# A four-layer hybrid transformer in fp32 on one core: the passage between sublayers in two halves of the tokens, with the last panel scaled in PSUM

## The chip, the cores and the metric

The kernel runs on one core of one Trainium2 chip. The metric is the device time of one execution in microseconds (us), median of the runs. The engines are TensorE (PE in the rows, PEld its weight loads), VectorE (DVE), ScalarE (ACT), GpSimd (POOL) and SyncE (SP), which here only starts DMAs.

## The reference

`h` is 512 tokens of 1024 features. Four layers each have a mixer (two kinds of attention with sparse or windowed keys, one stick-breaking attention) and a feed-forward part with a short convolution. Each of the eight sublayers is wrapped alike, and the change touches only the wrapping:

```python
def rms_norm(x, g):
    x32 = x.astype(jnp.float32)
    y = x32 * lax.rsqrt(jnp.mean(x32 * x32, axis=-1, keepdims=True) + RMS_EPS)
    return (y * g.astype(jnp.float32)).astype(x.dtype)
...
for layer in range(DEPTH):
    u = rms_norm(h, norm_g[layer, 0])
    u = mixer(u)                                # nsa, stick-breaking, swa, nsa; ends in "@ w_out"
    h = h + rms_norm(u, norm_g[layer, 1])
    u = conv_ffn(rms_norm(h, norm_g[layer, 2]), ...)  # ends in "@ w_down"
    h = h + rms_norm(u, norm_g[layer, 3])
```

## The kernel before

Features lie on the 128 partitions and tokens along the free dimension, so `h` is 8 chunks (`c`) of 128 x 512. Every fp32 product is made from three: weights and inputs are split into a rounded high part and a low part (`w_hi`, `w_lo`, `xh`, `xl`), and TensorE adds hi x hi, lo x hi and hi x lo. Weights come in units of 128 x 1024 through a ring of four buffers: SP loads `w_raw`, ScalarE rounds it (`split_hi`), VectorE subtracts (`split_lo`), TensorE uses it. A unit of an input projection covers two chunks and four banks of PSUM. A panel is four banks (512 output features) and takes four units; panels alternate between the two halves of PSUM, and `panel_free` waits until the panel two back was taken out (`evac_v`, `evac_s`).

The work around the change is the passage from the end of one sublayer (its output projection, two panels) to the first panel of the next. Each engine runs a list written out by hand, tied by semaphores. In order:

- `act_squares` squares each bank of the projection, `dve_take_u` copies each bank into `u` (`mix_u` or `ffn_u`), `pool_sum_squares` adds the first panel's squares, and `pe_post` sums over the partitions by products with `ones`, the last one after the projection's last bank.
- `act_rn` makes `rn` = (mean + eps)^-0.5 by Ln and Exp.
- `dve_update` goes through the eight chunks: scale `u` by the weight of the norm and by `rn` (line 454, into `dh`), add to `h` (line 460), and, one chunk behind, the low part `xl` = h * g - `xh` (line 440, `low`). Between them lies ScalarE's work of `act_update`: `xh`, the rounded h * g (line 472), and the square of `h` (line 477), which `pool_h_squares` adds up on GpSimd (lines 484 and 488).
- `first_panel` begins the next sublayer with what is there: it takes chunk by chunk, eight products with `xh` as soon as the chunk's `xh` is there (lines 319, 320), then four with `xl` (line 323). The division by the norm of `h` is left until after the products (`rb`), so `pe_rsum`, the sum over the squares, comes only after the first panel.
- The weights' units go on meanwhile: the fourth unit of the first panel is split on ScalarE behind the last square and on VectorE behind the last copy, ahead of the update.

There are eight such updates. Seven lead into another sublayer; the eighth has no `g_pre`, ends the kernel, and each chunk of `h` is written out by a DMA.

## Time and profile before

| | us |
|---|---|
| median of 3 runs | 2765.12 (2763.9 to 2768.2) |
| profiled execution, its own time | 2761.04 |
| its span, first to last instruction | 2759.3 |
| TensorE busy in it | 2629.6 |
| VectorE busy | 1721.9 |
| ScalarE busy | 1194.5 |
| GpSimd busy | 351.1 |

The times of single instructions come from the profiled execution. Starts in the rows are us from the span's start. A busy time counts an instruction from its start to its end, and TensorE's instructions overlap, so the distance from one start to the next tells more than a duration.

### The profile page before, as it was taken

The page shows a single profiled execution, that of the slowest core. Times are in us where ns is not written, and L with a number is a line of the kernel's source. Part 1 is how long each engine was busy: PE and PEld are TensorE (multiplying, and loading weights), DVE is VectorE, ACT ScalarE, POOL GpSimd, SP SyncE. Part 2 cuts the span into 40 slices and gives each one's busy share as a digit, 9 for nine tenths or more (in the row PEclk, how much of TensorE's full clock was granted, in tenths as well). Part 3 has the DMA queues.
Part 4 walks back from the last instruction along what each step waited for, and adds up shares of the span by engine and source line. Part 5 has one row for each costly group of instructions (what it writes and reads, how often), then busy time and mean ns, then how long its engine had stood idle before and what let it go on. Part 6 is the DMA issues. An engine that isn't in the chain of part 4 may idle for free.

```text
span 2759.3 us, 38755 instructions
## 1 busy us (share of the span) xinstructions
PE 2629.6 (95%) x13424; PEld 2201.1 (80%) x13424; DVE 1721.9 (62%) x2888; ACT 1194.5 (43%) x2117; POOL 351.1 (13%) x298
## 2 busy tenths in 40 slices
PE   8989999999999999999998999999999899999997
PEld 6878878888878787888877878888778788788886
DVE  7468857765262857767345767763476686676643
ACT  4356634443232744444235644443233665444431
POOL 1012211110010002111010021110011121211100
PEclk9989999999999999999999999999999999999999
DMA  4300023333223012332322023333333000233331
GB/s 159 122 31 2 2 69 99 99 92 98 85 96 100 16 39 77 100 99 84 107 74 69 14 87 100 99 92 99 96 100 100 9 2 24 77 103 96 99 96 49
DMA packets 62054, 210.93 MB, mean 76 GB/s; under 512 B 8672, under 2 KB 10464, under 8 KB 61920
## 3 DMA queue, kind: packets, MB, share of 16 engines
q1 hardware_dynamic: 61920, 209.14, 24.3%
q8 instruction: 84, 1.38, 0.2%
q14 instruction: 50, 0.41, 0.0%
HBM read 207.02 MB, written 2.10 MB: 76 GB/s over the span
## 4 chain that ended last, share of the span: by engine, by line
PE 83%; DVE 11%; ACT 3%; issue 2%; DMA 0%; DVEq 0%; POOL 0%; SPq 0%; ACTq 0%; POOLq 0%
PE psum L298 20%; PE psum L300 20%; PE psum L299 20%; PE psum L960 5%; PE psum L950 2%; DVE h L460 2%; PE psum L815 2%; PE psum L817 2%; PE psum L816 2%; PE psum L940 1%; DVE xl L440 1%; PE psum L319 1%; DVE qs L991 1%; PE psum L939 1%; PE psum L1701 1%
## 5 line engine op out<-in xcount | busy, mean ns | idle before, releaser
L298 PE MATMUL psum<-xh,w_hi 128*128 128x512 f32 x1736 | 682.2, 393 | 3.0 <-DVE xl L1204 3.0
L300 PE MATMUL psum<-xl,w_hi 128*128 128x512 f32 x1736 | 677.6, 390 | 0.0
L299 PE MATMUL psum<-xh,w_lo 128*128 128x512 f32 x1736 | 677.6, 390 | 0.0
L258 DVE TENSOR_TENSOR w_lo<-w_raw,w_hi 128x1024 fp32r<-128x1024 f32 x226 | 280.2, 1252 | 515.8 <-ACT w_hi L252 514.2
L252 ACT ACTIVATE w_hi<-w_raw 128x1024 fp32r<-128x1024 f32 x226 | 235.5, 1057 | 578.4 <-PE psum L300 456.0
L298 PEld LDWEIGHTS psum<-xh,w_hi 128*128 128x128 f32 x1736 | 327.3, 189 | 72.9 <-issue 5.8
L299 PEld LDWEIGHTS psum<-xh,w_lo 128*128 128x128 f32 x1736 | 327.3, 189 | 69.3 <-issue 1.9
L300 PEld LDWEIGHTS psum<-xl,w_hi 128*128 128x128 f32 x1736 | 327.0, 188 | 68.6
L615 DVE TENSOR_TENSOR w_lo<-w_raw,w_hi 128x1024 fp32r<-128x1024 f32 x160 | 209.2, 1308 | 253.8 <-ACT w_hi L611 253.8
L298 PE MATMUL psum<-ah,w_hi 128*128 (+1 forms) x704 | 277.1, 394 | 0.0
L300 PE MATMUL psum<-al,w_hi 128*128 (+1 forms) x704 | 274.0, 389 | 0.0
L299 PE MATMUL psum<-ah,w_lo 128*128 (+1 forms) x704 | 273.9, 389 | 0.0
L611 ACT ACTIVATE w_hi<-w_raw 128x1024 fp32r<-128x1024 f32 x160 | 168.5, 1053 | 234.9 <-PE psum L300 234.9
L960 PE MATMUL psum<-v,pt 128*128 128x64 f32 x1504 | 213.3, 272 | 25.4 <-DVE pt L1063 25.3
L960 PEld LDWEIGHTS psum<-v,pt 128*128 128x128 f32 x1504 | 203.3, 194 | 42.1 <-DVE pt L1063 37.1
L585 POOL TENSOR_TENSOR cv<-cv 128x512 f32<-128x512 f32 x88 | 133.7, 1519 | 787.0 <-ACT cv L539 784.3
L1114 ACT ACTIVATE scores<-scores,mins 128x256 f32<-128x256 f32 (+1 forms) x320 | 171.4, 538 | 29.6 <-DVE mins L1008 22.5
L534 ACT ACTIVATE cv<-xo,conv_b,conv_w 128x512 f32<-128x512 f32 x176 | 129.2, 805 | 95.5 <-DVE xo L558 95.5
L567 DVE SCALAR_TENSOR_TENSOR cv<-xo,conv_w,cv 128x512 f32<-128x512 f32 x176 | 169.5, 1003 | 0.6 <-DVE xo L558 0.6
L1008 DVE CUSTOM_DVE_ANT_0 scores<-psum,tb 128x256 f32<-128x256 f32 (+1 forms) x320 | 148.8, 468 | 25.0 <-PE psum L940 22.8
L299 PEld LDWEIGHTS psum<-ah,w_lo 128*128 128x128 f32 x704 | 132.2, 188 | 29.3 <-issue 1.9
L298 PEld LDWEIGHTS psum<-ah,w_hi 128*128 128x128 f32 x704 | 132.2, 188 | 29.2 <-issue 1.9
(180 smaller groups left out, 4011.1 us busy)
## 6 DMA issues: line engine op xcount, KB each, us to landing
w_raw<-w_up SPq DMA_DIRECT2D x176, 512.0 KB, 3.6
w_raw<-w_down SPq DMA_DIRECT2D x88, 512.0 KB, 3.6
w_raw<-nsa_in SPq DMA_DIRECT2D x56, 512.0 KB, 4.1
w_raw<-sb_in SPq DMA_DIRECT2D x24, 512.0 KB, 3.7
w_raw<-nsa_out SPq DMA_DIRECT2D x16, 512.0 KB, 3.6
w_raw<-swa_in SPq DMA_DIRECT2D x10, 512.0 KB, 4.4
w_raw<-sb_out SPq DMA_DIRECT2D x8, 512.0 KB, 3.6
w_raw<-swa_out SPq DMA_DIRECT2D x8, 512.0 KB, 3.8
```

The source lines that it names most:

```text
L252: nc.scalar.activation(w_hi[:, u % RING, :], w_raw[:, u % RING, :], ACT.Copy).then_inc(hi_done, 1)
L258: nc.vector.tensor_tensor(w_lo[:, u % RING, :], w_raw[:, u % RING, :], w_hi[:, u % RING, :].bitcast(F32), ALU.subtract).then_inc(split_don ...
L298: nc.tensor.matmul(bank(p, o), wh[:, k, o, :], xhi(k), start=(first and k == 0), stop=False)
L299: nc.tensor.matmul(bank(p, o), wl[:, k, o, :], xhi(k), start=False, stop=False)
L300: mm = nc.tensor.matmul(bank(p, o), wh[:, k, o, :], xlo(k), start=False, stop=(last and k == 1))
L567: marks.append(ch.then(nc.vector.scalar_tensor_tensor(cv[:, o, :], xo[:, o, 1:T + 1], conv_w[:, 1, bass.ds(cc, 1)], cv[:, o, :], ALU.mult, ...
L585: nc.gpsimd.tensor_tensor(cv[:, 2 + a, :], cv[:, a, :], cv[:, 2 + a, :], ALU.mult).then_inc(prod_done, 1)
L611: nc.scalar.activation(w_hi[:, u % RING, :], w_raw[:, u % RING, :], ACT.Copy).then_inc(hi_done, 1)
L615: nc.vector.tensor_tensor(w_lo[:, u % RING, :], w_raw[:, u % RING, :], w_hi[:, u % RING, :].bitcast(F32), ALU.subtract).then_inc(split_don ...
L960: mm = nc.tensor.matmul(psum[:, 6 + job % 2, i * DH:(i + 1) * DH], pt[:, s % 2, j * P:(j + 1) * P], vt[b][:, k0 + j, bass.ds(it * DH, DH)] ...
L1008: x = nc.vector.tensor_tensor_reduce(out=sp_[:, s % 4, 0:nk * P], in0=psum[:, s % 4, 0:nk * P], in1=bias, scale=1.0, scalar=3e38, op0=ALU. ...
L1114: nc.scalar.activation(sp_[:, s % 4, 0:nk * P], sp_[:, s % 4, 0:nk * P], ACT.Exp, scale=-1.0, bias=mins[:, c:c + 1], accum_out=rsums[:, c: ...
```

## The change

The passage is arranged anew:

- The last bank's square, the sum over the partitions, Ln and Exp are made in two halves of 256 tokens. The mean of the squares comes from `ones` that hold 1/D, so Ln needs no scale. The halves lie in two banks (`mean_half`).
- Chunk 0's `xh` no longer comes from ScalarE. ScalarE prepares h * g_pre of the old `h` ahead of the second panel's squares (`hg_done`); VectorE scales `u` by `gg` (the product of both norms' weights, made once at the start) and by `rn` and adds the prepared part, rounding as it writes `xh`, half by half. `first_panel` takes chunk 0's products with `xh` in halves.
- VectorE's order in `dve_update` is new: `xh` of chunk 0 in halves, update of chunk 1, update of chunk 0, both low parts, then for each chunk from 2 on the update and its low part. An update is line 454's scaling and line 460's add, the second waiting for the first.
- The second panel is not copied out: chunks 4 to 7 are scaled in place in PSUM, and the panel counts as taken out (`evac_v`) at the end of the update.
- VectorE's split of the first panel's fourth unit moves from ahead of the update to behind the update of chunk 4. ScalarE's stays.

```diff
+TH = T // 2
...
+        gg = small("gg", [P, 2 * DEPTH - 1], F32)
...
-        mix_u = Space(A_, T_)("mix_u", [P, DC, T], F32)
-        ffn_u = Space(16 * K, 32 * K)("ffn_u", [P, DC, T], F32)
+        mix_u = Space(A_, T_)("mix_u", [P, 4, T], F32)
+        ffn_u = Space(24 * K, 32 * K)("ffn_u", [P, 4, T], F32)
...
+        sqa_done = sem("sqa_done")
+        hg_done = sem("hg_done")
+        xa_done = sem("xa_done")
+        gg_done = sem("gg_done")
-        dh_done = sem("dh_done")
...
                 for k in range(2):
                     c = 2 * j + k
-                    pe.wait_ge(xh_done, 8 * n + c + 1)
-                    pe.wait_ge(split_done, u + 1)
-                    for o in range(4):
-                        nc.tensor.matmul(bank(p, o), wh[:, k, o, :], xh[:, c, :], start=(c == 0), stop=False)
-                        nc.tensor.matmul(bank(p, o), wl[:, k, o, :], xh[:, c, :], start=False, stop=False)
+                    parts = [(0, T)] if c or n == 0 else [(0, TH), (TH, T)]
+                    for lo, hi in parts:
+                        if hi < T:
+                            pe.wait_ge(xa_done, n)
+                        else:
+                            pe.wait_ge(xh_done, 8 * n + c + 1)
+                        pe.wait_ge(split_done, u + 1)
+                        for o in range(4):
+                            if o == 3 and hi < T:
+                                pe.wait_ge(r_done, 2 * n)
+                            nc.tensor.matmul(bank(p, o)[:, lo:hi], wh[:, k, o, :], xh[:, c, lo:hi], start=(c == 0 and lo == 0), stop=False,
+                                             skip_group_check=True)
+                            nc.tensor.matmul(bank(p, o)[:, lo:hi], wl[:, k, o, :], xh[:, c, lo:hi], start=False, stop=False,
+                                             skip_group_check=True)
                     pe.wait_ge(x_ready, 8 * n + c + 1)
                     for o in range(4):
-                        mm = nc.tensor.matmul(bank(p, o), wh[:, k, o, :], xl[:, c, :], start=False, stop=(c == DC - 1))
+                        mm = nc.tensor.matmul(bank(p, o), wh[:, k, o, :], xl[:, c, :], start=False, stop=(c == DC - 1),
+                                              skip_group_check=True)
                 mm.then_inc(units_done, 1)
 
         def after_rsum(pe, p, u0, n, by_token):
...
-                act.wait_ge(s_chain, ch.then(nc.scalar.activation(rt[:], bank(p, 2)[:, 0:TC], ACT.Ln, bias=eps[:], scale=1.0 / D)))
+                act.wait_ge(s_chain, ch.then(nc.scalar.activation(rt[:], bank(p, 2)[:, 0:TC], ACT.Ln, bias=eps[:])))
...
-            a = nc.scalar.activation(rb[:], bank(p, 3), ACT.Ln, bias=eps[:], scale=1.0 / D)
+            a = nc.scalar.activation(rb[:], bank(p, 3), ACT.Ln, bias=eps[:])
...
             if o == 2:
                 panel_free(pe, p + 1)
                 pe.wait_ge(ss_done, s + 1)
-                nc.tensor.matmul(bank(p + 1, 3), ones[:], ss[:], start=True, stop=False)
+                for a in range(2):
+                    nc.tensor.matmul(mean_half(p, a), ones[:], ss[:, TH * a:TH * a + TH], start=True, stop=False)
             for c in ((), (), (0,), (1,), (2, 3))[o]:
-                pe.wait_ge(sq_done, 8 * s + 5 + c)
-                mm = nc.tensor.matmul(bank(p + 1, 3), ones[:], sq[:, c, :], start=False, stop=(c == 3))
-            if o == 4:
-                mm.then_inc(ssum_done, 1)
+                for a in range(2):
+                    if c == 3 and a == 0:
+                        pe.wait_ge(sqa_done, s + 1)
+                    else:
+                        pe.wait_ge(sq_done, 8 * s + 5 + c)
+                    mm = nc.tensor.matmul(mean_half(p, a), ones[:], sq[:, c, TH * a:TH * a + TH], start=False, stop=(c == 3))
+                    if c == 3:
+                        mm.then_inc(ssum_done, 1)
+
+        def mean_half(p, a):
+
+            return bank(p + 1, 2 + a)[:, 0:TH]
 
         def act_squares(act, s, half, p, u_end):
 
             if half:
                 act.wait_ge(ss_done, s + 1)
+                if s < 2 * len(kinds) - 1:
+                    nc.scalar.activation(dh[:, 1, :], h[:, 0, :], ACT.Copy, scale=norm_g[:, 2 * s + 2, 0:1]).then_inc(hg_done, 1)
             for o in range(4):
                 if o < 3:
                     act.wait_ge(bank_done, 6 * s + 3 * half + o + 1)
                 else:
                     act.wait_ge(units_done, u_end)
-                nc.scalar.activation(sq[:, o, :], bank(p, o), ACT.Square).then_inc(sq_done, 1)
-
-        def dve_take_u(dve, s, p, half, u):
+                if half and o == 3:
+                    nc.scalar.activation(sq[:, 3, 0:TH], bank(p, 3)[:, 0:TH], ACT.Square).then_inc(sqa_done, 1)
+                    nc.scalar.activation(sq[:, 3, TH:T], bank(p, 3)[:, TH:T], ACT.Square).then_inc(sq_done, 1)
+                else:
+                    nc.scalar.activation(sq[:, o, :], bank(p, o), ACT.Square).then_inc(sq_done, 1)
+
+        def dve_take_u(dve, s, p, u):
             for o in range(4):
-                dve.wait_ge(sq_done, 8 * s + 4 * half + o + 1)
-                nc.vector.tensor_copy(u[:, 4 * half + o, :], bank(p, o)).then_inc(u_done, 1)
-            dve.wait_ge(u_done, 8 * s + 4 * half + 4)
+                dve.wait_ge(sq_done, 8 * s + o + 1)
+                nc.vector.tensor_copy(u[:, o, :], bank(p, o)).then_inc(u_done, 1)
+            dve.wait_ge(u_done, 4 * s + 4)
...
         def act_rn(act, ch, s, p):
-            act.wait_ge(ssum_done, s + 1)
-            act.wait_ge(s_chain, ch.then(nc.scalar.activation(rn[:], bank(p + 1, 3), ACT.Ln, bias=eps[:], scale=1.0 / D)))
-            nc.scalar.activation(rn[:], rn[:], ACT.Exp, scale=-0.5).then_inc(r_done, 1)
-
-        def dve_update(dve, s, u, g_post, g_pre):
+            for a in range(2):
+                half = slice(TH * a, TH * a + TH)
+                act.wait_ge(ssum_done, 2 * s + a + 1)
+                act.wait_ge(s_chain, ch.then(nc.scalar.activation(rn[:, half], mean_half(p, a), ACT.Ln, bias=eps[:])))
+                nc.scalar.activation(rn[:, half], rn[:, half], ACT.Exp, scale=-0.5).then_inc(r_done, 1)
+
+        def dve_update(dve, ch, s, u, p, u_split, g_post, g_pre):
...
                     if c % 2:
                         split_lo(dve, c // 2)
                 return
-            dve.wait_ge(r_done, s + 1)
-            for c in range(DC):
-                if c >= 2:
-                    dve.wait_ge(h_done, 8 * s + c - 1)
-                nc.vector.scalar_tensor_tensor(dh[:, c % 2, :], u[:, c, :], norm_g[:, g_post, c:c + 1],
-                                               rn[:], ALU.mult, ALU.mult).then_inc(dh_done, 1)
-                if c and g_pre is not None:
-                    dve.wait_ge(h_done, 8 * s + c)
-                    low(c - 1)
-                dve.wait_ge(dh_done, 8 * s + c + 1)
-                nc.vector.tensor_tensor(h[:, c, :], h[:, c, :], dh[:, c % 2, :], ALU.add).then_inc(h_done, 1)
-            if g_pre is not None:
+
+            def update(c):
+                if c < 4:
+                    src, d = u[:, c, :], dh[:, c % 2, :]
+                else:
+                    src = d = bank(p, c - 4)
+                dve.wait_ge(v_chain, ch.then(nc.vector.scalar_tensor_tensor(d, src, norm_g[:, g_post, c:c + 1], rn[:], ALU.mult, ALU.mult)))
+                nc.vector.tensor_tensor(h[:, c, :], h[:, c, :], d, ALU.add).then_inc(h_done, 1)
+
+            for a in range(2):
+                half = slice(TH * a, TH * a + TH)
+                dve.wait_ge(r_done, 2 * s + a + 1)
+                if g_pre is not None:
+                    dve.wait_ge(v_chain, ch.then(nc.vector.scalar_tensor_tensor(dh[:, 0, half], u[:, 0, half], gg[:, s:s + 1], rn[:, half],
+                                                                                ALU.mult, ALU.mult)))
+                    dve.wait_ge(hg_done, s + 1)
+                    x = nc.vector.tensor_tensor(xh[:, 0, half], dh[:, 0, half], dh[:, 1, half], ALU.add)
+                    if a == 0:
+                        x.then_inc(xa_done, 1)
+                    else:
+                        x.then_inc(xh_done, 1)
+            if g_pre is None:
+                for c in range(DC):
+                    if c >= 2:
+                        dve.wait_ge(h_done, 8 * s + c - 1)
+                    update(c)
                 dve.wait_ge(h_done, 8 * s + DC)
-                low(DC - 1)
+                dve.sem_inc(evac_v, 1)
+                return
+            dve.wait_ge(xh_done, 8 * (s + 1) + 1)
+            update(1)
+            update(0)
+            dve.wait_ge(h_done, 8 * s + 2)
+            low(0)
+            low(1)
+            for c in range(2, DC):
+                update(c)
+                if c == 4:
+                    split_lo(dve, u_split)
+                dve.wait_ge(h_done, 8 * s + c + 1)
+                low(c)
+            dve.sem_inc(evac_v, 1)
 
         def act_update(act, s, g_pre, first_units=False):
 
-            for c in range(DC):
-                if s < 0:
-                    act.wait_ge(x_landed[c // 2], 16)
-                else:
-                    act.wait_ge(h_done, 8 * s + c + 1)
+            def high(c):
                 nc.scalar.activation(xh[:, c, :], h[:, c, :], ACT.Copy, scale=norm_g[:, g_pre, c:c + 1]).then_inc(xh_done, 1)
+
+            def square(c):
                 if c >= 4:
                     act.wait_ge(ssh_done, 8 * (s + 1) + c - 3)
-                elif s >= 0:
-                    act.wait_ge(ssum_done, s + 1)
                 nc.scalar.activation(sq[:, c % 4, :], h[:, c, :], ACT.Square).then_inc(sqh_done, 1)
-                if first_units and c % 2:
-                    split_hi(act, c // 2)
+
+            if s < 0:
+                for c in range(DC):
+                    act.wait_ge(x_landed[c // 2], 16)
+                    high(c)
+                    square(c)
+                    if first_units and c % 2:
+                        split_hi(act, c // 2)
+                return
+            act.wait_ge(xh_done, 8 * (s + 1) + 1)
+            act.wait_ge(h_done, 8 * s + 1)
+            high(1)
+            act.wait_ge(h_done, 8 * s + 2)
+            square(0)
+            square(1)
+            for c in range(2, DC):
+                act.wait_ge(h_done, 8 * s + c + 1)
+                high(c)
+                square(c)
...
-            dve_take_u(dve, s, plan.down_p[l], 0, ffn_u)
+            dve_take_u(dve, s, plan.down_p[l], ffn_u)
             split_los(dve, d0 + FC // 2 + 2, FC // 2 - 2)
-            dve_take_u(dve, s, plan.down_p[l] + 1, 1, ffn_u)
-            split_lo(dve, d0 + FC + AHEAD)
...
-            dve_take_u(dve, 2 * l, plan.out_p[l], 0, mix_u)
+            dve_take_u(dve, 2 * l, plan.out_p[l], mix_u)
             split_los(dve, u + 6, 2)
-            dve_take_u(dve, 2 * l, plan.out_p[l] + 1, 1, mix_u)
-            split_lo(dve, u + 8 + AHEAD)
...
             nc.vector.memset(eps[:], EPS)
-            nc.vector.memset(ones[:], 1.0).then_inc(ones_set, 1)
-            dve_update(dve, -1, None, None, 0)
+            nc.vector.memset(ones[:], 1.0 / D).then_inc(ones_set, 1)
+            dve.wait_ge(consts_landed, 32)
+            nc.vector.tensor_tensor(gg[:], norm_g[:, 1:15:2, 0:1].rearrange("p s o -> p (s o)"),
+                                    norm_g[:, 2:16:2, 0:1].rearrange("p s o -> p (s o)"), ALU.mult).then_inc(gg_done, 1)
+            dve.wait_ge(gg_done, 1)
+            dve_update(dve, ch, -1, None, None, None, None, 0)
             for l, kind in enumerate(kinds):
                 last = l == len(kinds) - 1
                 if kind:
                     dve_mixer(dve, ch, l, kind)
-                    dve_update(dve, 2 * l, mix_u, 4 * l + 1, 4 * l + 2)
+                    dve_update(dve, ch, 2 * l, mix_u, plan.out_p[l] + 1, plan.up_u[l] + AHEAD, 4 * l + 1, 4 * l + 2)
                 s = per * l + per - 1
                 dve_ffn(dve, ch, l, s, s)
-                dve_update(dve, s, ffn_u, 4 * l + 3, None if last else 4 * l + 4)
+                dve_update(dve, ch, s, ffn_u, plan.down_p[l] + 1, plan.down_u[l] + FC + AHEAD, 4 * l + 3, None if last else 4 * l + 4)
```

## Rows read from the trace of the kernel before

**Rows 1.** The page: its span, and the chain that ended last, by engine.
```profile
span 2759.3 us, 38755 instructions
...
PE 83%; DVE 11%; ACT 3%; issue 2%; DMA 0%; DVEq 0%; POOL 0%; SPq 0%; ACTq 0%; POOLq 0%
```

**Rows 2.** Line 472 (`xh`): who waited for it (us, times).
```profile
  PE psum L319: 29.6, 15
```

**Rows 3.** Timeline of ScalarE, passage at 394: start, us, what [idle before, releaser].
```profile
394.70 0.60 ACT L411 ACTIVATE sq<-psum 128x512 f32<-128x512 f32 x1 [1.64 <-PE psum L300]
395.19 1.05 ACT L252 ACTIVATE w_hi<-w_raw 128x1024 fp32r<-128x1024 f32 x1
396.51 0.69 ACT L433 ACTIVATE rn<-psum,eps 128x512 f32<-128x512 f32 x1 [0.27 <-PE psum L398]
397.23 0.63 ACT L434 ACTIVATE rn<-rn 128x512 f32<-128x512 f32 x1
399.41 0.72 ACT L472 ACTIVATE xh<-h,norm_g 128x512 fp32r<-128x512 f32 x1 [1.55 <-DVE h L460]
...
406.69 0.62 ACT L477 ACTIVATE sq<-h 128x512 f32<-128x512 f32 x1
...
417.79 0.72 ACT L472 ACTIVATE xh<-h,norm_g 128x512 fp32r<-128x512 f32 x1 [2.06 <-DVE h L460]
...
421.11 0.72 ACT L472 ACTIVATE xh<-h,norm_g 128x512 fp32r<-128x512 f32 x1 [2.07 <-DVE h L460]
```

**Rows 4.** Timeline of VectorE, same passage.
```profile
396.27 1.23 DVE L258 TENSOR_TENSOR w_lo<-w_raw,w_hi 128x1024 fp32r<-128x1024 f32 x1 [0.25 <-ACT w_hi L252]
397.89 0.75 DVE L454 SCALAR_TENSOR_TENSOR dh<-mix_u,norm_g,rn 128x512 f32<-128x512 f32 x1 [0.40 <-ACT rn L434]
398.68 0.69 DVE L460 TENSOR_TENSOR h<-h,dh 128x512 f32<-128x512 f32 x1
399.29 0.75 DVE L454 SCALAR_TENSOR_TENSOR dh<-mix_u,norm_g,rn 128x512 f32<-128x512 f32 x1
400.24 0.75 DVE L440 SCALAR_TENSOR_TENSOR xl<-h,norm_g,xh 128x512 fp32r<-128x512 f32 x1 [0.20 <-ACT xh L472]
400.91 0.69 DVE L460 TENSOR_TENSOR h<-h,dh 128x512 f32<-128x512 f32 x1
...
406.89 0.75 DVE L440 SCALAR_TENSOR_TENSOR xl<-h,norm_g,xh 128x512 fp32r<-128x512 f32 x1 [0.20 <-ACT xh L472]
407.56 1.78 DVE L460 TENSOR_TENSOR h<-h,dh 128x512 f32<-128x512 f32 x1
409.26 1.78 DVE L454 SCALAR_TENSOR_TENSOR dh<-mix_u,norm_g,rn 128x512 f32<-128x512 f32 x1
```

**Rows 5.** Timeline of TensorE, same passage: first products of chunks 0, 2, 3, 7.
```profile
400.39 0.72 PE L319 MATMUL psum<-xh,w_hi 128*128 128x512 f32 x1 [3.91 <-ACT xh L472]
...
407.55 0.39 PE L319 MATMUL psum<-xh,w_hi 128*128 128x512 f32 x1
...
410.27 0.39 PE L319 MATMUL psum<-xh,w_hi 128*128 128x512 f32 x1
...
421.88 0.50 PE L319 MATMUL psum<-xh,w_hi 128*128 128x512 f32 x1 [0.30 <-ACT xh L472]
```

**Rows 6.** Timeline of GpSimd, same passage.
```profile
407.45 1.34 POOL L484 TENSOR_TENSOR ss<-sq 128x512 f32<-128x512 f32 x1 [25.29 <-ACT sq L477]
408.93 4.97 POOL L488 TENSOR_TENSOR ss<-ss,sq 128x512 f32<-128x512 f32 x3
```

**Rows 7.** VectorE instructions that read PSUM: ns min/median/max, first and last start.
```profile
L1008 DVE CUSTOM_DVE_ANT_0 scores<-psum,tb x320: 282/422/692, 173.9 to 2314.1; 128x256 f32<-128x256 f32 x96, 128x512 f32<-128x512 f32 x64
...
L874 DVE SCALAR_TENSOR_TENSOR qt<-psum,rb x24: 673/680/693, 65.5 to 2086.7; 128x512 f32<-128x512 f32 x24
```

**Rows 8.** Timeline of ScalarE, passage at 767: Ln and the rounding of chunk 7.
```profile
767.57 0.69 ACT L433 ACTIVATE rn<-psum,eps 128x512 f32<-128x512 f32 x1 [0.27 <-PE psum L398]
...
792.51 0.72 ACT L472 ACTIVATE xh<-h,norm_g 128x512 fp32r<-128x512 f32 x1 [2.07 <-DVE h L460]
```

## The prediction

> **What bounds the kernel now.** I read the page first. The chain that ended last is TensorE for 83% and VectorE for 11% [rows 1], so TensorE sets the time wherever it isn't starved. The places to look for are those where it is. The row of line 472 says where: TensorE's first products of a chunk waited 29.6 us for `xh`, in 15 instructions [rows 2]. These lie in the passages between sublayers. There are seven that lead into another sublayer, and an eighth at the end that only updates `h`.
>
> Then the timelines of one passage, engine by engine. I count from T, the start of the last square of the projection, at 394.70. The chain to TensorE's first product is: the norm's sum, Ln at T+1.81, Exp at T+2.53 [rows 3], VectorE's scaling at T+3.19 and add at T+3.98 [rows 4], ScalarE's rounding at T+4.71 [rows 3], first product at T+5.69 [rows 5].
>
> The decisive reading is at the other end of the panel. Undisturbed, TensorE spends 2.72 us on a chunk (407.55 to 410.27), but the last chunk starts only at T+27.18, 0.77 us after the rounding of chunk 7 at T+26.41, and it had waited [rows 3, 5]. So the panel ends when the chain VectorE to ScalarE delivers chunk 7, and an earlier start of chunk 0 alone gives nothing. Why is that chain slow? Alone, VectorE and ScalarE make a chunk in about 2.2 us: from an add 0.73 to the rounding (398.68, 399.41), 0.83 to the low part of line 440 (400.24), 0.67 to the next add (400.91), 2.23 in all [rows 3, 4]. But once GpSimd adds squares (from 407.45 on [rows 6]) a VectorE instruction behind a GpSimd one takes 1.78 instead of 0.7 us and holds the next back: 407.56 to 409.26 is 1.70 [rows 4]. Late in the panel one such instruction falls on each chunk, and a chunk takes 3.32 us (417.79 to 421.11 [rows 3]). That is above TensorE's 2.72. The passage's end is therefore a matter of VectorE's order of work and of how often it meets GpSimd.
>
> **The change, part by part.** I follow the new VectorE order to the rounding of chunk 7 and compare it with T+26.41.
>
> *Front, in halves.* Half of an instruction saves its 256 columns. From VectorE's 1024-column 1.23 against 512-column 0.69 a half saves about 0.27 [rows 4]; from ScalarE's 1.06 against 0.60, about 0.23 [rows 3] (other operations, so estimates). The two halves of square 3 start at T and about T+0.3, the split of the weights at T+0.6. It occupies ScalarE to about T+1.6, and this, not the sum (its first half is there one 0.43 earlier than T+1.81, so at about T+1.4), sets the first Ln. Ln a 1.6, Exp a 2.1, Ln b 2.45, Exp b 2.95, done 3.35. VectorE: scaling a T+2.5, `xh` a T+3.05, done 3.45. ScalarE's rounding is off this path, and TensorE begins near T+3.7 instead of 5.69: 2.0 us earlier. The second half follows at T+3.4 and 3.9, finished at T+4.35.
>
> *Chunks 1 and 0.* VectorE now scales and adds chunk 1 at T+4.35 and 5.15, chunk 0 at 5.75 and 6.55 (scaling to dependent add 0.79, add to next 0.61 [rows 4]), then waits for its own add and does the low parts at 7.3 and 7.95, and can scale chunk 2 at T+8.6. The low part of chunk 0 is later than before (T+5.54), so TensorE, through with the halves by about T+6.8, waits until about T+8.3. The 2.0 us are mostly given back here.
>
> *Chunks 2 to 7.* Before, the next scaling filled the 0.83 us in which ScalarE rounds. Now scaling, add, wait for ScalarE, low part follow one another: 0.79 + 0.73 + 0.83 + 0.67 = 3.0 us a chunk in place of 2.23. For c >= 4 the scaling reads and writes PSUM. The rows have no VectorE instruction that writes PSUM; from PSUM to SBUF the same operation takes 0.68 against 0.75 [rows 4, 7]. I take 0.68, that is 2.94 a chunk; bounds 0.62 (as much less again) and 0.75. Roundings: chunk 2 T+10.15, chunk 3 T+13.15, add of chunk 4 T+15.35.
>
> *GpSimd.* It starts after the fourth square, which begins 0.20 ahead of the low part (406.69, 406.89), and the add 0.76 after that (407.45) [rows 3, 4, 6]. The low part of chunk 3 is at T+13.97, so GpSimd starts at T+14.55. Does it block operands in PSUM? In the rows line 1008 reads PSUM and one table in SBUF beside GpSimd's work of the attention, 320 times, and none took over 0.692 [rows 7]. So I take scaling and adds of chunks 4 to 7 as free. The scaling of chunk 4 also writes PSUM, which no row shows. The Trainium skill ("SBUF — State Buffer", Who interferes with whom) says that a VectorE instruction with at most one SBUF input doesn't contend with GpSimd, whatever it writes; only the maximum just named bears that out here.
>
> Still exposed are the weights' split (1024 columns, moved to after the update of chunk 4) and the low parts. The split is due at T+15.98; GpSimd's second add at 14.55 + 1.48 = T+16.0 (407.45 to 408.93 [rows 6]). Which wins? A VectorE instruction 0.56 ahead of GpSimd ran free (406.89), one 0.11 behind it was held (407.56) [rows 4, 6]. At 0.02 ahead we are much nearer to the held row, and I take GpSimd as first. Then the split is held by about 1.08, the low part of chunk 4 behind it too, by the third add. Sum: low part 4 at T+18.3, scaling 5 at 20.0, add 20.75, rounding 5 at 21.45. From here GpSimd comes 0.6 after each low part and meets only PSUM work, so 2.94 a chunk: roundings at 24.4 and **T+27.35**. TensorE's last chunk starts 0.77 later and the panel ends 0.94 us later than before.
>
> If VectorE wins, the split is free, the low part of chunk 4 is held to T+19.0, and the low part of chunk 5 meets the next add for 0.25 to 0.45: rounding 7 at T+26.5, or +0.1.
>
> *What hides at nothing.* The prepared residual (0.72 on ScalarE ahead of the second half's squares) lies in time in which ScalarE waits for TensorE; the first square would start about 0.3 later and still be ahead of its consumer. If that cover were gone it would cost 0.3 to 0.7 per passage. The four copies removed were hidden too, since VectorE was idle before T+3.19. Splitting the products with `ones` moves no columns. The `gg` product is once and tiny. The panel's bank is released only after all low parts, near T+29; who waits is the norm sum behind the first panel, which TensorE reaches later. The moved split frees `w_raw` about 16 us later; SP's next load, one of SP's queue in order, then starts near T+18.4 in place of T+2.8; its unit is wanted in the second panel, after T+31, so 12 us are left for the load, and it is hidden. Unit 3 of the first panel is wanted for chunk 6, near T+25, and is ready at T+18.4.
>
> *The eighth passage.* No GpSimd, no low parts. Exp b ends about 0.2 later than the old Exp, four scalings in PSUM save about 0.06 each: 0.0, bounds -0.3 and +0.3.
>
> **Sum.** Six passages at +0.94. In the passage at 767 the old chain lost time once: its chunk 7 was rounded 24.94 after Ln against 24.60 [rows 3, 8], so +0.6 there. 6 x 0.94 + 0.6 = +6.2 us. The profiled execution took 2761.04 us, 1.7 beyond its span of 2759.3 [rows 1]; the median of the runs is 2765.12, and I add to that: 2771.3 us, +0.23%. About 0.2% (5.5 us) is what a measurement of this kernel can tell from no change.
>
> **The rivals.**
> 1. *VectorE wins the start of the split.* Everything else stands. Six passages at +0.1, one at -0.25: about 2765.5, no change. For it: the two starts are 0.02 us apart. Against: the held row is the nearer one.
> 2. *The panel really ends earlier.* Its one mechanism is GpSimd's place: if VectorE met GpSimd nowhere in the panel, the rounding of chunk 7 would come at T+25.1 (split 15.98, low part 17.13, scaling 17.8, add 18.5, rounding 19.25, two chunks at 2.94), and TensorE 1.3 us earlier, 8.7 us in seven: 2756. It decides from about 0.8 us per passage, so both held instructions must fall away. For it: all of the late chunks are on PSUM. Against: the split and the low part of chunk 4 stand in the middle of three adds in a row.
> 3. *GpSimd blocks PSUM operands that are written back as well, or all of them.* Then scaling and add of chunk 4, split, low part 4 and one instruction in each of the chunks 5 and 6 are held, six by 1.05 us: T+31.4, 5 us a passage, 2800. Against: the row of line 1008.
> 4. *PSUM is the dearer operand.* The Trainium skill ("VectorE: DVE Perf Modes", The TRN2 errata) gives a fixed cost of 120 cycles with a PSUM source against 58 from SBUF. By it (an estimate, at the same page's 0.96 GHz) each of the two instructions would be 65 ns longer than from SBUF, where the row makes the scaling 65 ns shorter. As a mechanism of this kernel, from rows: should a scaling in place take 0.75 + 0.07 and the add 0.69 + 0.07, the roundings slip 0.2 a chunk, 0.8 at chunk 7, and the end is 2777. The page's rule gives about that too. The 0.68 speaks against it; the trace of before has no in-place row.
>
> **How the numbers follow.** Forecast 0.45 (own range 2768 to 2774), VectorE wins 0.27, earlier end 0.12, PSUM blocked 0.04, PSUM dearer 0.06, and 0.06 for a cover that fails (0.5 us a passage on top, 2775). The forecast's own bound cuts near the 0.2% line, 2770.6: 0.27 of its 0.45 above, 0.18 below. Slower: 0.27 + 0.04 + 0.06 + 0.05 (of the failing cover) = 0.42. Same: 0.18, 0.25 of rival 1 and 0.01 of the cover's, 0.44. Faster: 0.12 and 0.02 of rival 1, 0.14. The range takes in the forecast, rival 1 and the near parts of rivals 2 and 4: 2760 to 2776.
>
> **What would show it.** In the changed profile: TensorE's first product of the panel near T+3.7; a wait of TensorE for the low part of chunk 0, until about T+8.3; scaling and add of chunks 4 to 7 at 0.68 with GpSimd running; the split after chunk 4 at 2.3 us (held) or 1.23 (free), which tells the forecast from rival 1; 2.9 to 3.0 us between late roundings in place of 3.3; and the rounding of chunk 7 at T+27.3. The prediction is wrong if that last number is below T+26, if TensorE does not wait for chunk 7 at all, or if any scaling in PSUM shows 1.7 us.

## The result, and the profile after

| | before | changed |
|---|---|---|
| median, us | 2764.70 (2763.9 to 2768.2, 4 runs) | 2786.66 (2781.57 to 2788.06, 4 runs) |
| profiled span, us | 2759.3 | 2783.4 |

The ratio is 1.0075, 95% interval 1.006 to 1.009: slower by about 21 us. The forecast was 2771.3 us, the range 2760 to 2776. "Slower" had a chance of 0.42; the size lies outside the range.

The page after, its span and its chain by engine, beside [rows 1]:

```profile
span 2783.4 us, 39063 instructions
...
PE 83%; DVE 11%; ACT 3%; issue 2%; DMA 0%; DVEq 0%; POOL 0%; SPq 0%; ACTq 0%; POOLq 0%
```

The chain looks the same and doesn't help. The row of line 331 (the products of a chunk's `xh` with `w_hi`, line 319 before) does. Who ended TensorE's idle time ahead of it (us, times), and one start on TensorE's timeline in the passage at 765:

```profile
  DVEq L525: 53.5, 2
...
  DVE xh L500: 11.9, 6
  ACT xh L530: 10.7, 21
```
```profile
794.03 0.58 PE L331 MATMUL psum<-xh,w_hi 128*128 128x256 f32 x1 [26.53 <-DVEq L525]
```

Line 525 is the `evac_v` at the end of `dve_update`. In one passage, that into the stick-breaking layer, TensorE waited 26.5 us for it (the row counts the weight load and the product, hence 53.5). In the six others it came to its first product as forecast. The passage at 393, with T as in the prediction, the start of the last square (here its first half, T = 393.75). ScalarE's timeline:

```profile
393.75 0.39 ACT L438 ACTIVATE sq<-psum 128x256 f32<-128x256 f32 x1 [1.66 <-PE psum L305]
394.03 0.38 ACT L439 ACTIVATE sq<-psum 128x256 f32<-128x256 f32 x1
394.29 1.06 ACT L257 ACTIVATE w_hi<-w_raw 128x1024 fp32r<-128x1024 f32 x1
395.24 0.48 ACT L465 ACTIVATE rn<-psum,eps 128x256 f32<-128x256 f32 x1
...
418.14 0.73 ACT L530 ACTIVATE xh<-h,norm_g 128x512 fp32r<-128x512 f32 x1 [1.76 <-DVE h L491]
...
421.14 0.72 ACT L530 ACTIVATE xh<-h,norm_g 128x512 fp32r<-128x512 f32 x1 [1.76 <-DVE h L491]
```

VectorE's, at chunks 4 and 5:

```profile
408.26 0.75 DVE L490 SCALAR_TENSOR_TENSOR psum<-psum,norm_g,rn 128x512 f32<-128x512 f32 x1
409.05 0.69 DVE L491 TENSOR_TENSOR h<-h,psum 128x512 f32<-128x512 f32 x1
409.65 2.36 DVE L263 TENSOR_TENSOR w_lo<-w_raw,w_hi 128x1024 fp32r<-128x1024 f32 x1
411.94 1.78 DVE L474 SCALAR_TENSOR_TENSOR xl<-h,norm_g,xh 128x512 fp32r<-128x512 f32 x1
413.64 0.75 DVE L490 SCALAR_TENSOR_TENSOR psum<-psum,norm_g,rn 128x512 f32<-128x512 f32 x1
```

GpSimd's, beside them:

```profile
408.15 1.34 POOL L559 TENSOR_TENSOR ss<-sq 128x512 f32<-128x512 f32 x1 [26.95 <-ACT sq L535]
409.64 5.23 POOL L563 TENSOR_TENSOR ss<-ss,sq 128x512 f32<-128x512 f32 x3
```

And TensorE's, the first product and the first low product of chunk 0, the norm sum behind the panel:

```profile
397.39 0.36 PE L331 MATMUL psum<-xh,w_hi 128*128 128x256 f32 x1 [1.96 <-DVE xh L500]
...
401.73 0.50 PE L337 MATMUL psum<-xl,w_hi 128*128 128x512 f32 x1 [2.20 <-DVE xl L474]
...
424.80 1.02 PE L385 MATMUL psum<-ss,ones 128*128 128x512 f32 x2
```

To be seen: first product at T+3.64 in place of T+5.69 [rows 5], then an idle stretch of 2.20 us for `xl`; the rounding of chunk 7 at T+27.39 in place of T+26.41 [rows 3]; 3.0 us between the last two; the norm sum at T+31.05 (T+30.04 before). The split and the low part of chunk 4 are held by GpSimd, 2.36 and 1.78 us. The scaling and the add of chunk 4 (408.26, 409.05) run while GpSimd's first add does (408.15 to 409.49) and take 0.75 and 0.69: what works in PSUM is not held.

**The sum over the passages.** From the norm sums (start of line 370 before, 385 after, each from its T): about +1.0 us (0.9 to 1.0) in five passages, 0.0 in the one at 2009, and 52.30 against 30.39 at 765, +21.9. Together 26.9. The spans differ by 24.1. The other 2.8 lie outside the passages: the stretch from the norm sum of the passage at 765 to the next T took 252.5 us after and 255.4 before, the first sublayer was 0.95 shorter, the one behind the passage at 1442 was 1.1 longer. In the stick-breaking attention, which lies in the first of these, the granted clock was 0.99 after and 0.95 before. That is not the work of the wait: the same stretch took 252.8, 253.0 and 252.9 us in three of the runs below in which TensorE waits for no release (all passages copied, the order filled, TensorE takes chunk 1 first), 255.4 with the split early and 257.1 with one passage copied. It differs from one profiled execution to the next by more than most effects in a passage, and what sets it stays open. So the passages are compared by their own start and end, and the totals over many runs.

### The profile page after: what moved, and what is told of

It reads as the page before. It is cut to its first block, busy times and chain, and to the rows that moved or that the text cites. A ratio compares the mean times of both kernels' runs of the same rounds, so it can differ in the third digit from the quotient of the medians.

```text
span 2783.4 us, 39063 instructions
## 1 busy us (share of the span) xinstructions
PE 2631.9 (95%) x13560; PEld 2219.7 (80%) x13560; DVE 1684.2 (61%) x2885; ACT 1196.1 (43%) x2141; POOL 353.8 (13%) x298
## 4 chain that ended last, share of the span: by engine, by line
PE 83%; DVE 11%; ACT 3%; issue 2%; DMA 0%; DVEq 0%; POOL 0%; SPq 0%; ACTq 0%; POOLq 0%
PE psum L303 20%; PE psum L304 20%; PE psum L305 20%; PE psum L1033 5%; PE psum L1023 2%; PE psum L888 2%; PE psum L890 2%; PE psum L889 2%; PE psum L331 1%; PE psum L337 1%; PE psum L333 1%; PE psum L1013 1%; DVE h L491 1%; PE psum L1012 1%; DVE qs L1064 1%
## 5 line engine op out<-in xcount | busy, mean ns | idle before, releaser
L263 DVE TENSOR_TENSOR w_lo<-w_raw,w_hi 128x1024 fp32r<-128x1024 f32 x226 | 286.8, 1281 | 535.0 <-ACT w_hi L257 533.5
L690 DVE TENSOR_TENSOR w_lo<-w_raw,w_hi 128x1024 fp32r<-128x1024 f32 x160 | 209.3, 1308 | 253.8 <-ACT w_hi L686 253.8
L1187 ACT ACTIVATE scores<-scores,mins 128x256 f32<-128x256 f32 (+1 forms) x320 | 171.4, 538 | 29.2 <-DVE mins L1081 22.4
L331 PE MATMUL psum<-xh,w_hi 128*128 128x512 f32 (+1 forms) x284 | 113.9, 405 | 51.1 <-DVEq L525 26.5
L1023 PE MATMUL psum<-ident,scores 128*128 128x128 f32 x752 | 142.6, 285 | 12.9 <-ACT scores L1187 12.5
```

What stands on the lines that cost most here:

```text
L263: nc.vector.tensor_tensor(w_lo[:, u % RING, :], w_raw[:, u % RING, :], w_hi[:, u % RING, :].bitcast(F32), ALU.subtract).then_inc(split_don ...
L690: nc.vector.tensor_tensor(w_lo[:, u % RING, :], w_raw[:, u % RING, :], w_hi[:, u % RING, :].bitcast(F32), ALU.subtract).then_inc(split_don ...
L1023: mm = nc.tensor.transpose(psum[:, 4 + s % 2, j * P:(j + 1) * P], sp_[:, s % 4, j * P:(j + 1) * P], ident[:])
L1187: nc.scalar.activation(sp_[:, s % 4, 0:nk * P], sp_[:, s % 4, 0:nk * P], ACT.Exp, scale=-1.0, bias=mins[:, c:c + 1], accum_out=rsums[:, c: ...
```

## The experiments

The ratio of a run is to the kernel before, timed again beside it. The T of each passage is the start of the last square in that run's own trace.

**One passage copied.** The second panel of the passage into the stick-breaking layer (s = 1, so `copied` is [1]) is copied out and released early.

```diff
+        def dve_take_v(dve, s, p, v):
+            if s not in copied:
+                return
+            for o in range(4):
+                dve.wait_ge(sq_done, 8 * s + 4 + o + 1)
+                nc.vector.tensor_copy(v[:, o, :], bank(p, o)).then_inc(v_done, 1)
+            dve.wait_ge(v_done, 4 * copied.index(s) + 4)
+            dve.sem_inc(evac_v, 1)
...
+                elif s in copied:
+                    src, d = (ffn_v if s % 2 else mix_v)[:, c - 4, :], dh[:, c % 2, :]
...
-            dve.sem_inc(evac_v, 1)
+            if s not in copied:
+                dve.sem_inc(evac_v, 1)
```

> The changed kernel, but in the one passage into the stick-breaking layer the second panel is copied out to SBUF and released early, as before. Theory (the late release starves TensorE there, because that layer's first panel lies in the same half of PSUM as the panel that VectorE still scales): TensorE's first product comes near T+3.7 instead of T+28.2 and that passage's panel ends about 21 us earlier; the total is 19 to 22 us below the changed kernel, 0 to +0.25% against the kernel before. Rival (something else holds TensorE in that passage, the release only carries the label): the total stays above +0.6%.

Measured: 2772.04 us, ratio 1.0029 (1.0016 to 1.0043). TensorE's timeline in that passage (T = 767.35), and the norm sum of the panel at T+35.02:

```profile
771.00 0.36 PE L335 MATMUL psum<-xh,w_hi 128*128 128x256 f32 x1 [1.96 <-DVE xh L515]
```

The 26.5 us are gone. The passage still ends 4.6 us later than before and not at +1, because its chunks 4 to 7 now have two operands in SBUF (next run). The total went down by 0.46% of the kernel before, about 13 us, against the 17.3 us of that passage. The expected 19 to 22 us were missed, and so, barely, was the 0 to 0.25% above before: the expectation had left out what the copied chunks cost. The remainder above before, 0.29% or 8 us, fits the passages: +4.6, four times +1.0, and twice 0.0.

**All passages copied.** The same with copied = all eight.

> The changed kernel with the second panel copied out in all eight passages, so that VectorE scales and adds chunks 4 to 7 from SBUF. Theory (operands in PSUM are free of GpSimd, two operands in SBUF are not): scalings and adds of chunks 4 to 6 now take 1.8 us where a GpSimd add runs, up to four more held instructions a passage, the rounding of chunk 7 at T+29 to T+31.5 instead of T+27.4, total 2778 to 2797. Rival (scaling in PSUM buys nothing): rounding of chunk 7 stays at T+27.4, total as in the run with one passage copied.

Measured: 2795.61 us, ratio 1.0119 (1.0099 to 1.0138). The rounding of chunk 7 comes at T+31.4 in all seven passages (31.36 to 31.42), as expected. VectorE, GpSimd and that rounding in the passage with T = 394.98:

```profile
409.50 1.79 DVE L505 SCALAR_TENSOR_TENSOR dh<-mix_v,norm_g,rn 128x512 f32<-128x512 f32 x1
411.32 1.67 DVE L506 TENSOR_TENSOR h<-h,dh 128x512 f32<-128x512 f32 x1
412.91 2.31 DVE L267 TENSOR_TENSOR w_lo<-w_raw,w_hi 128x1024 fp32r<-128x1024 f32 x1
415.14 1.76 DVE L487 SCALAR_TENSOR_TENSOR xl<-h,norm_g,xh 128x512 fp32r<-128x512 f32 x1
```
```profile
409.39 1.34 POOL L576 TENSOR_TENSOR ss<-sq 128x512 f32<-128x512 f32 x1 [26.95 <-ACT sq L552]
410.88 3.25 POOL L580 TENSOR_TENSOR ss<-ss,sq 128x512 f32<-128x512 f32 x2
```
```profile
426.40 0.72 ACT L547 ACTIVATE xh<-h,norm_g 128x512 fp32r<-128x512 f32 x1 [2.79 <-DVE h L506]
```

Scaling in PSUM is worth 4.0 us a passage, and all of it is GpSimd: the same scaling takes 0.75 in PSUM and 1.79 from SBUF, each 0.11 us behind the start of a GpSimd add. Six VectorE instructions are held here before the rounding of chunk 7 (scaling and add of chunk 4, split, low part of chunk 4, scalings of chunks 5 and 6) where two are in the changed kernel, four more at about 1.0 us each. "Scaling in PSUM buys nothing" falls. The Trainium skill ("SBUF — State Buffer", Who interferes with whom) says that a VectorE instruction with two SBUF inputs contends with a GpSimd instruction that reads SBUF, and that one with at most one, outside the two-port modes, does not. These two kernels agree, 1.79 against 0.75 us, with an output in PSUM too.

**The old kernel with a late release.** One part of the change alone.

```diff
             dve.wait_ge(u_done, 8 * s + 4 * half + 4)
-            dve.sem_inc(evac_v, 1)
+            if not (s == 1 and half == 1):
+                dve.sem_inc(evac_v, 1)
...
                 low(DC - 1)
+            if s == 1:
+                dve.sem_inc(evac_v, 1)
```

> The kernel before, with one edit: in the passage into the stick-breaking layer the second panel counts as taken out only at the end of VectorE's update. Theory: TensorE's first product there waits to about T+28.5 and the panel ends about 22 us later, total +0.7 to +0.85% against before, nearly the whole loss of the change from this alone. Rival (late release matters only together with the new order or the halves): under +0.3%.

Measured: 2777.82 us, ratio 1.0058 (1.0039 to 1.0077). TensorE in that passage (T = 764.00), its norm sum at T+51.41 against T+30.39:

```profile
791.49 0.80 PE L319 MATMUL psum<-xh,w_hi 128*128 128x512 f32 x1 [25.71 <-DVEq L466]
```

The wait comes back with nothing else changed: 21.0 us in the passage, 16 us in the total, where 0.7 to 0.85% had been expected. In the profiled execution, of what is missing, 2.9 us lie between this norm sum and the next T, a stretch of 252.5 us as in the changed kernel, and 1.8 ahead of the first passage. The windows of the attention before the next T, before and in this run (columns: window, its length, busy us and count of PE, PEld, DVE, ACT, POOL, then the granted clock as a share of full speed, DMA share, GB/s):

```profile
905.90:1051.50 145.60, 137.43 (x844) 109.50 (x843) 96.81 (x154) 86.04 (x156) 3.94 (x3) 0.95 0.11 32
```
```profile
922.30:1067.90 145.60, 135.93 (x857) 107.64 (x856) 99.14 (x158) 86.59 (x157) 3.95 (x3) 0.99 0.10 33
```

The faster stretch is no answer to the wait, since three runs without the wait have it too (252.8 to 253.0 us, above). In the totals the late release alone is about three quarters of the loss (0.58% of 0.75%, each to about 0.2%), and in the passage 21.0 of 21.9 us.

**The split early.** As the run with one passage copied, and:

```diff
             low(1)
+            split_lo(dve, u_split)
             for c in range(2, DC):
                 update(c)
-                if c == 4:
-                    split_lo(dve, u_split)
```

> As the run with one passage copied, and VectorE's split of the fourth unit stands ahead of the update of chunk 2, before GpSimd begins. Theory (the split and the low part of chunk 4 are held by GpSimd's adds, 1.1 us each): split 1.23 us, low part of chunk 4 held by 0.2 at most or not, rounding of chunk 7 near T+26.5, 0.8 us a passage and 5 us in all below that run. Rival (the split's own length sets it, wherever it stands): rounding of chunk 7 at T+27.4 or later.

Measured: 2764.98 us, ratio 1.0015 (1.0000 to 1.0029). Against the run with one passage copied that is 4 us less by the ratios and 7 by the medians; expected were 5. VectorE in the passage with T = 394.42, and ScalarE's rounding of chunk 7:

```profile
402.94 1.22 DVE L267 TENSOR_TENSOR w_lo<-w_raw,w_hi 128x1024 fp32r<-128x1024 f32 x1
...
412.41 0.89 DVE L487 SCALAR_TENSOR_TENSOR xl<-h,norm_g,xh 128x512 fp32r<-128x512 f32 x1 [0.86 <-ACT xh L546]
```
```profile
420.86 0.72 ACT L546 ACTIVATE xh<-h,norm_g 128x512 fp32r<-128x512 f32 x1 [1.76 <-DVE h L506]
```

Split free, low part of chunk 4 held by 0.14, rounding of chunk 7 at T+26.44 (26.42 to 26.45) in the six passages. The intervals of the two runs overlap, so the totals don't tell them apart; the roundings do, equal in every passage. The norm sums of the seven passages add up to 3.8 us less than in that run.

**The order filled.** One passage copied, the split ahead of the update, behind the second panel's copies, and the next chunk's scaling back into VectorE's wait for ScalarE:

```diff
+            split_lo(dve, d0 + FC + AHEAD)
...
+            ahead = scale(2)
             low(0)
             low(1)
             for c in range(2, DC):
-                update(c)
-                if c == 4:
-                    split_lo(dve, u_split)
+                add(c, ahead)
+                if c < DC - 1:
+                    dve.wait_ge(h_done, 8 * s + c)
+                    ahead = scale(c + 1)
                 dve.wait_ge(h_done, 8 * s + c + 1)
                 low(c)
```

> As the run with one passage copied, with two edits of VectorE's order: the scaling of the next chunk stands again between the add and the low part of this one, in the time in which ScalarE rounds, and the split of the fourth unit stands ahead of the update. Theory (3.0 us a chunk instead of 2.2 is what the new order costs, and VectorE's chain is what ends the panel): rounding of chunk 7 near T+23.3 instead of T+27.4, the panel then ends with TensorE's own work, its norm sum near T+29.2 against T+30.04 before and T+31.05 changed; total 0.1 to 0.3% below before. Rival (GpSimd takes it all back): rounding of chunk 7 at T+26 or later, no gain.

Measured: 2763.28 us, ratio 1.0008 (0.9998 to 1.0018). The expected gain of 0.1 to 0.3% was missed. VectorE did what was expected, the rounding of chunk 7 at T+23.14, 4.2 us earlier than in the changed kernel. The panel didn't: the norm sum at T+30.69, where T+29.2 was expected (five common passages from 29.1 to 30.7, one 31.8). ScalarE and TensorE in the passage with T = 394.88:

```profile
418.02 0.72 ACT L555 ACTIVATE xh<-h,norm_g 128x512 fp32r<-128x512 f32 x1 [0.96 <-DVE h L509]
```
```profile
403.86 1.19 PE L341 MATMUL psum<-xl,w_hi 128*128 128x512 f32 x4 [2.86 <-DVE xl L487]
404.89 0.44 PE L335 MATMUL psum<-xh,w_hi 128*128 128x512 f32 x1
405.13 0.63 PE L337 MATMUL psum<-xh,w_lo 128*128 128x512 f32 x1
405.55 0.63 PE L335 MATMUL psum<-xh,w_hi 128*128 128x512 f32 x1
...
409.23 0.39 PE L335 MATMUL psum<-xh,w_hi 128*128 128x512 f32 x1
409.45 0.40 PE L337 MATMUL psum<-xh,w_lo 128*128 128x512 f32 x1
```

After 2.86 us of idling the products of chunk 1 follow at 0.43 us, then at 0.23: TensorE's lower and its full clock level. The low stretch costs eight products some 1.6 us. The expectation had not counted them.

The passage with T = 1988.48 is the counterpart within the same run. There TensorE was at the lower level earlier, in chunk 0's half products, which have time to spare since `xl` of chunk 0 comes only at T+8.98 either way. After the wait, the products ran at 0.23, and the norm sum came at T+29.06, near the expected 29.2. The windows from T to the norm sum (columns as above), and TensorE behind the wait:

```profile
394.88:425.57 30.69, 25.55 (x112) 20.87 (x111) 24.91 (x32) 15.35 (x25) 9.88 (x7) 0.94 0.13 38
1988.48:2017.54 29.06, 25.36 (x112) 21.18 (x111) 24.74 (x32) 15.36 (x25) 11.01 (x9) 0.94 0.33 106
```
```profile
1997.46 1.19 PE L341 MATMUL psum<-xl,w_hi 128*128 128x512 f32 x4 [1.41 <-DVE xl L487]
1998.49 0.40 PE L335 MATMUL psum<-xh,w_hi 128*128 128x512 f32 x1
1998.72 0.39 PE L337 MATMUL psum<-xh,w_lo 128*128 128x512 f32 x1
```

The mean granted clock is the same 0.94, so it is the place of the low stretch that makes the 1.6 us. With VectorE's chain last, such stretches had cost nothing (the kernel before was granted 0.89 to 0.94 in each passage up to its norm sum, and these came at T+30.0 to T+30.4 all the same). Now the panel ends with TensorE, whose wait for `xl` of chunk 0 is on the path.

**The order filled, and TensorE takes chunk 1 first.**

```diff
+                    if n and j == 0 and k == 0:
+                        continue
+                    for kk in (0, 1) if n and j == 0 else (k,):
+                        c = 2 * j + kk
+                        pe.wait_ge(x_ready, 8 * n + c + 1)
+                        for o in range(4):
+                            mm = nc.tensor.matmul(bank(p, o), wh[:, kk, o, :], xl[:, c, :], start=False, stop=(c == DC - 1),
+                                                  skip_group_check=True)
```

> As the run before it, and in the first panel TensorE takes the eight high products of chunk 1 ahead of the low products of chunk 0. Theory (TensorE's wait for the low part of chunk 0, T+5.5 to T+9, eats the earlier start): chunk 1 begins near T+7.1, the norm sum comes near T+27.4, total 0.45 to 0.7% below the kernel before. Rival (VectorE's chain binds in the middle of the panel, at chunks 4 to 6): norm sum at T+28.5 or later, under 0.35% below.

Measured: 2748.92 us, ratio 0.9961 (0.9947 to 0.9975). TensorE in the passage with T = 394.62, then the windows from T to the norm sum of this run and of the kernel before (columns as above):

```profile
401.57 0.50 PE L335 MATMUL psum<-xh,w_hi 128*128 128x512 f32 x1 [0.74 <-ACT xh L559]
...
422.08 1.02 PE L393 MATMUL psum<-ss,ones 128*128 128x512 f32 x2
```
```profile
394.62:422.00 27.38, 24.27 (x112) 19.54 (x111) 23.06 (x31) 15.36 (x25) 9.88 (x7) 1.00 0.06 20
```
```profile
394.70:424.70 30.00, 25.79 (x100) 19.45 (x99) 25.97 (x27) 15.17 (x23) 10.24 (x7) 0.94 0.07 19
```

The idle stretch of 2.86 us became one of 0.74, the clock stayed at full level (1.00, against 0.94 in the filled order and before), and the norm sum comes at T+27.46, as expected and 2.6 us ahead of before. In two of the six common passages TensorE was at the lower level around chunk 0's half products (0.94), and their norm sums came at T+27.5 all the same. This version beats both kernels. The total, 0.39% (0.25 to 0.53), fell short of the expected 0.45 to 0.7% mainly for the one copied passage, whose norm sum is at T+31.10, 0.7 behind before. Of the 3.2 us against the filled order, the clock makes 1.6, as the passage at 1988 shows (T+30.69 against T+29.06), and the new order the other 1.6 (T+29.06 against T+27.46).

## Why the prediction was wrong

- **The release of the bank: the step that failed.** "The panel's bank is released only after all low parts, near T+29; who waits is the norm sum behind the first panel, which TensorE reaches later." That holds where the next first panel lies in the other half of PSUM than the second panel. `pe_sb` starts at `plan.mix_p[l] + 1` and leaves a panel out (the (0, 0) at the head of its `MIX_READS`), so its first panel lies in the same half. `panel_free` then waits for exactly the release that the change moves behind the update. The timeline of one passage, which is of the common kind, stood for seven, and the wait of TensorE's first product stood in the sum at nothing. Measured: a wait of 26.5 us in that passage, which ended 21.9 us later. The old kernel with only the release late shows the cause: +21.0 us there.
- **The rest of the sum held, in part by luck.** For the others the forecast was +0.94 or, if VectorE won the start of the split, +0.1. Measured: about +1.0 in five, 0.0 in one. First product T+3.64 (3.7), `xl` of chunk 0 awaited until T+7.98 (8.3), rounding of chunk 7 at T+27.39 (27.35). Without the one passage the changed kernel would have been near 2770 by the passages (2764.7 and 5), or 2765 by the medians (2786.7 less 21.9); the run with one passage copied bears out the sum over the passages, 8 us where they give 8.6.
- **Rival 1** was no alternative to the forecast but a coin tossed in every passage. In the one at 2009 the split and GpSimd's second add start at the same rounded 0.01 us, and VectorE went first; in five others the add's start is 0.01 to 0.02 us ahead, and GpSimd did:

```profile
2024.95 1.22 DVE L263 TENSOR_TENSOR w_lo<-w_raw,w_hi 128x1024 fp32r<-128x1024 f32 x1
```
```profile
2024.95 5.51 POOL L563 TENSOR_TENSOR ss<-ss,sq 128x512 f32<-128x512 f32 x3
```

- **Rival 3** (PSUM operands blocked) fell, though the row against it was weaker than it was read: of line 1008's 320 instructions only 124 overlap one of GpSimd's in the trace of before. The changed kernel's own rows decide it (0.75 and 0.69 us beside GpSimd). Its sum of six held instructions, T+31.4, is what the kernel with all passages copied measured. **Rival 2** fell: two instructions were held. **Rival 4** was right in a part: scaling in place takes 0.75, as from SBUF, where the row from PSUM to SBUF had 0.68 and I took that. It made 3.0 us a chunk instead of 2.94, and an Ln 0.1 earlier than worked out cancelled it, by luck. The add with an operand in PSUM took 0.69, as from SBUF, so the 65 ns that the rival's rule adds for a source in PSUM show in neither instruction.
- **The eighth passage** ended 16.8 us after its T in both kernels: nothing, as forecast.
- **The range.** No rival had a wait of TensorE for a PSUM bank; the 0.06 for "a cover that fails" was priced at 0.5 us a passage. When a change moves a release, every one who waits on that semaphore is to be looked up, in each kind of layer. The wait is bounded by the length of the work that the release was moved past; here it was 26.5 us, and the passage ended 21.9 us later.

## What to carry to other kernels

Scaling the last panel in place in PSUM keeps VectorE clear of GpSimd, but it makes the bank's release as late as the update; look in every kind of stage at which panel takes that bank next. An earlier first product is worth nothing while the chain that delivers the last chunk is as late as before: count that chain to its end first, and put independent work into its waits. Then see what TensorE does with the earlier start, since an idle stretch in the middle costs its length and, where the clock falls behind it, more (here 1.6 us).

## What the runs showed of the hardware

- The clock after idling in a passage: behind a wait of 2.86 us, in three of three passages, the clock fell about a microsecond after the work had begun again, and eight products ran at 0.43 us instead of 0.23; behind one of 0.74 to 0.84 us none did, in the four common passages that have it. Equal waits don't make an equal clock: in the run with one passage copied, the passages with T = 395.31 and T = 1059.45 both have waits of 1.96 and 2.2 us, and were granted 0.94 and 1.00.
- The same low stretch costs 1.6 us or nothing, as it falls on TensorE's work behind its last wait (norm sum T+30.69) or ahead of it (T+29.06), at the same mean clock of 0.94.
- The stretch with the stick-breaking layer, the same products in all of them, took 252.5 to 253.0 us in five of eight profiled executions, 255.4 in two and 257.1 in one. In its attention the granted clock was 0.99 in the changed kernel and 0.95 in the kernel before. A wait of 26 us ahead of it is not the cause, since three of the five have none; the cause is open.
- A VectorE instruction with two operands in SBUF and a GpSimd add whose starts lie within 0.02 us of each other: either can go first, and the other is held for about 1.1 us (split of 1.22 or 2.36 us). With one operand in PSUM the VectorE instruction was not held 0.11 us behind the add's start (0.75 us).
